# A decoder layer whose feed-forward products are made as seven block products of 2x2 blocks

## What is computed

```python
x = x + rmsnorm(concat(window_attention(...), pool_mix(...)) @ w_out, g_post)
h = rmsnorm(x, g_pre_ffn)
a = jnp.square(jax.nn.relu(h @ w_up))      # w_up   (2048, 8192)
y = x + rmsnorm(a @ w_down, g_post_ffn)    # w_down (8192, 2048)
```

## Time and profile before

| | |
|---|---|
| runs, median (lowest to highest) | 2207.6 us (2205.54 to 2207.78) |
| profiled execution, span | 2207.5 us |
| TensorE busy | 2151.8 us, 97% |
| VectorE, ScalarE, POOL busy | 966.5, 533.8 and 149.3 us |
| mean granted clock of TensorE | 0.979 |
| chain that ended last | TensorE 94%, VectorE 4% |

### The profile page before, as it was taken

How to read it: one execution, slowest core, us unless ns; L and a number is a source line. 1 busy time by engine, 2 the same in 40 slices (tenths; PEclk the granted TensorE clock), 3 DMA queues, 4 the chain that set the end, 5 groups by cost and what they waited for, 6 DMA issues and landing times.

```text
span 2207.5 us, 39376 instructions
## 1 busy us (share of the span) xinstructions
PE 2151.8 (97%) x16878; PEld 2123.3 (96%) x16878; DVE 966.5 (44%) x1212; ACT 533.8 (24%) x743; POOL 149.3 (7%) x135
## 2 busy tenths in 40 slices
PE   7999999999889999999999999999999999999996
PEld 7999989999889999999999999999999999999995
DVE  3455436322574344343434444343344434334446
ACT  5244414222231212121121212112121112212132
POOL 0000023100350000000000000000000000000024
PEclk9999989999889999999999999999999999999996
DMA  5421112522112222222223222222222222222222
GB/s 174 148 64 52 58 58 67 180 86 86 57 48 86 87 90 91 86 86 86 86 85 95 86 86 86 88 90 85 88 86 86 88 93 86 86 86 86 86 67 81
DMA packets 181548, 192.70 MB, mean 87 GB/s; under 512 B 6080, under 2 KB 177480, under 8 KB 180911
## 3 DMA queue, kind: packets, MB, share of 16 engines
q1 hardware_dynamic: 178016, 181.96, 26.2%
q10 hardware_dynamic: 3479, 9.99, 1.2%
HBM read 186.95 MB, written 7.37 MB: 88 GB/s over the span
## 4 chain that ended last, share of the span: by engine, by line
PE 94%; DVE 4%; DMA 0%; issue 0%; ACT 0%; SPq 0%; POOL 0%; DVEq 0%; ACTq 0%; POOLq 0%
PE banks L1271 89%; PE banks L1416 1%; DVE acts_lo L1138 1%; DVE x1T L1213 1%; PE banks L1237 1%; PE banks L1386 1%; DVE x1T L1143 1%; PE banks L1404 1%; DVE w_lo L808 1%; DMA x_tok<-in_x_sample 0%; PE banks L1458 0%; PE banks L1245 0%; PE banks L1457 0%; DVE k_twice L871 0%; DVE x1T L1147 0%
## 5 line engine op out<-in xcount | busy, mean ns | idle before, releaser
L808 DVE TENSOR_TENSOR w_lo<-w_raw,w_hi 128x1024 fp32r<-128x1024 f32 x330 | 421.4, 1277 | 688.6 <-ACT w_hi L545 685.0
L1271 PE MATMUL banks<-acts_hi,w_hi 128*128 128x272 f32 x3232 | 681.2, 292 | 17.3 <-DVE acts_lo L1138 5.3
L1271 PE MATMUL banks<-acts_hi,w_lo 128*128 128x272 f32 x3232 | 674.2, 290 | 0.0
L1271 PE MATMUL banks<-acts_lo,w_hi 128*128 128x272 f32 x3232 | 671.9, 290 | 0.0
L545 ACT ACTIVATE w_hi<-w_raw 128x1024 fp32r<-128x1024 f32 x330 | 349.3, 1059 | 1305.6 <-PE banks L1271 1298.6
L1271 PEld LDWEIGHTS banks<-acts_hi,w_hi 128*128 128x128 f32 x3232 | 512.9, 190 | 24.9 <-issue 14.8
L1271 PEld LDWEIGHTS banks<-acts_lo,w_hi 128*128 128x128 f32 x3232 | 513.6, 191 | 0.0
L1271 PEld LDWEIGHTS banks<-acts_hi,w_lo 128*128 128x128 f32 x3232 | 510.2, 191 | 0.0
L1271 PE MATMUL banks<-mlp_lo,w_hi 128*128 128x272 f32 x2048 | 424.8, 288 | 0.0
L1271 PE MATMUL banks<-mlp_hi,w_hi 128*128 128x272 f32 x2048 | 422.5, 287 | 0.0
L1271 PE MATMUL banks<-mlp_hi,w_lo 128*128 128x272 f32 x2048 | 422.3, 287 | 0.0
(11 more groups left out here) (187 smaller groups left out, 732.6 us busy)
## 6 DMA issues: line engine op xcount, KB each, us to landing
w_raw<-in_w_up SPq DMA_DIRECT2D x128, 512.0 KB, 3.6
w_raw<-in_w_down SPq DMA_DIRECT2D x128, 512.0 KB, 3.3
w_raw<-in_w_in SPq DMA_DIRECT2D x40, 512.0 KB, 3.6
w_raw<-in_w_out SPq DMA_DIRECT2D x32, 512.0 KB, 3.4
x_tok<-in_x_prompt SPq DMA_DIRECT2D x8, 512.0 KB, 9.1
x_tok<-in_x_prompt ACTq DMA_DIRECT2D x4, 1024.0 KB, 8.0
out<-w_raw SPq DMA_DIRECT2D x16, 256.0 KB, 2.6
old_k<-in_cache_k ACTq DMA_DIRECT2D x1, 1024.0 KB, 19.5
```

Of the source, the lines that this page charges most:

```text
L808: nc.vector.tensor_tensor(w_lo[:, k % SPLIT_SLOTS, :], w_raw[:, k % RAW_SLOTS, :], w_hi[:, k % SPLIT_SLOTS, :].bitcast(F32), ALU.subtract) ...
L1271: ins = nc.tensor.matmul(out[:, h, :], w, x[:, h * H:(h + 1) * H], start=first, stop=last)
```

## The change

The two feed-forward products are no longer made chunk by chunk. Each operand is seen as 2x2 blocks: the inner dimension by even and odd tiles of 128, the output columns by the two tiles of a pair, the rows by the two halves of 272. Of each group the four weight blocks b11, b12, b21, b22 and four activation blocks are combined to seven products instead of eight, each with its own high and low parts (Winograd's form of Strassen's scheme):

- POOL makes four differences of weight blocks per group: t1 = b12 - b11, t3 = b22 - b12, t2 = b22 - t1, t4 = b21 - t2 (buffers `t_x`, `t_z`, `t_y`). The sums of activation blocks are made once for the up product by VectorE (`h_sums`), and for the down product by POOL (`activation_sums`).
- For each product N ScalarE copies the weights twice with rounding, once to PSUM (`high_copy`, banks 4 to 7) and once to SBUF (`high_part`); VectorE subtracts the PSUM copy from the weights (`low_part`).
- `take` adds each finished product from its PSUM bank (one of 0 to 3, 272 columns) into the block sums `quads` or `y_sum`. Some products are accumulated on top of what the bank holds, and `taken_before` says which takes TensorE awaits.
- There are two passes. The up pass has 32 groups of 7 products of 8 x 3 matmuls; after each, relu and square (`square_relu`), POOL's sums, rounding (`mlp_high`), rest (`mlp_low`), and two stores to DRAM (`mlp_kept`). The down pass has 8 chunks of 8 groups of 7 products of 4 x 3 matmuls, and reads the parts back (`load_part`). Raw weights have two buffers of 2 MB in the up pass, three of 1 MB in the down pass.
- The input is scaled before the first product (`scale_tiles`), so all tiles are turned and summed before it. x1 is stored to DRAM and read back in the last chunk.
- The loops of the out-projection and the feed-forward are written out; SBUF is laid out by hand.

```diff
+        BANK = (None, 3, None, 2, None, 2, None)
+        GOES_TO = (0, 0, 1, 3, 3, 1, 2)
+        T_NEEDS = {2: 3, 3: 1, 4: 2, 6: 4}
...
+            def load_part(c, i):
+                sp.dma_start(mlp_parts[:, c % 2, i].bitcast(F32),
+                             mlp_kept[c * DOWN_J:(c + 1) * DOWN_J, :, KEPT_AT[i]].rearrange("j p h n -> p j h n")
+                             ).then_inc(mlp_landed[i], 16)
...
+            for g in range(UP_GROUPS):
+                if g > 0:
+                    store_hi(g - 1)
+                    store_lo(g - 1)
...
+            for i in range(NP):
+                sp.wait_ge(product_done, N_UP - NP + i // 2 + 1)
+                load_part(0, i)
...
+            def t4(G):
+                gp.wait_ge(part_hi, NP * G + 3)
+                gp.wait_ge(part_lo, NP * G + 3)
+                gp.wait_ge(t_ready, 4 * G + 3)
+                nc.gpsimd.tensor_tensor(t_of(G, t_y), block_of(G, 1, 0), t_of(G, t_y), ALU.subtract).then_inc(t_ready, 1)
...
+            def high_part(N):
+                if split_free(N):
+                    act.wait_ge(product_done, split_free(N))
+                nc.scalar.activation(split_of(N, 0), weight_of(N), ACT.Copy).then_inc(part_hi, 1)
...
+            for N in range(4, N_ALL):
+                high_copy(N)
+                high_part(N)
+                G, i = divmod(N, NP)
+                if i == 4 and 0 < G < UP_GROUPS:
+                    mlp_high(G - 1)
...
+            for N in range(3, N_UP):
+                take(N)
+                if N < N_UP - 3:
+                    low_part(N + 3)
...
+                if i == 2 and G > 0:
+                    mlp_low(G - 1)
+                if i == 6:
+                    square_relu(G)
...
+            def taken_before(G, i):
...
+                last_group = NP * (G - 1)
+                return (last_group, last_group + 2, NP * G + 1, last_group + 6, NP * G + 3, NP * G + 4, NP * G + 5)[i]
...
+            def strassen_product(N):
+                G, i = divmod(N, NP)
+                pe.wait_ge(part_hi, N + 1)
+                pe.wait_ge(part_lo, N + 1)
+                if taken_before(G, i) > 0:
+                    pe.wait_ge(taken, taken_before(G, i))
...
+                for j in range(pairs):
...
+                    nc.tensor.matmul(out, wh, xh, start=first, stop=False, skip_group_check=not STARTS[i])
+                    nc.tensor.matmul(out, wh, xl, start=False, stop=False, skip_group_check=not STARTS[i])
+                    ins = nc.tensor.matmul(out, wl, xh, start=False, stop=j == pairs - 1, skip_group_check=not STARTS[i])
+                ins.then_inc(product_done, 1)
```

More of the change, by code:

```diff
@@ L40 @@
 UNIT_N = 256
+SB_BASE = 16512
+SB_END = 229344
 POOL_WINDOWS = (2, 4, 8, 16)
@@ L533, in _ @@
+            add(2, KT - 2, sqf_sum, sqf_tmp)
             gp.wait_ge(scale_ready, 4)
@@ L1206, in _ @@
+            for N in range(N_UP, N_ALL):
+                take(N)
+                if N + 4 < N_ALL:
+                    low_part(N + 4)
+                if N == N_UP + 3:
+                    mlp_low(UP_GROUPS - 1)
+            row_scales(3, norm_f)
             dve.wait_ge(scale_ready, 4)
+            for one in x1_moved:
+                dve.wait_ge(one, 32)
             def finish_tiles(kg):
```

740 lines of the change are left out of this document (490 added, 250 removed).

## The result

The changed kernel takes 2095.4 us (median of four runs, 2095.1 to 2096.8) against 2207.7 us before (2205.5 to 2208.5): ratio 0.949, 95% interval 0.948 to 0.951. The forecast was 2091 with 2050 to 2150. The profiled execution has a span of 2095.1 us, 112.4 less than the one before.

The account below looks back on a forecast made before the run. TensorE, busy 97% of the span, was taken as the bound, by its number of matmuls. 2207.5 - 192.3 (matmuls) + 28 (up-pass chain) + 37 (handover) + 10 (between passes) + 1 (tail) = 2091 us, range 2050 to 2150.

Parts of the forecast that it names:

- Step 1: Feed-forward matmuls on TensorE: 1536 fewer at an unchanged 125.2 ns each, -192.3 us.
- I am wrong if the pace of matmuls itself moves: Sign against the forecast: the feed-forward's time per matmul, kept at 125.2 ns, changes.
- Step 2: Down pass: work of VectorE, ScalarE and POOL fits beside TensorE's 1.5 us products, cost 0.
- Step 3: Up pass: one chain across VectorE, POOL and ScalarE makes TensorE wait 0.9 us per group, +28 us.
- The prediction's 0.3: Up-pass chain: overlap in us of a VectorE and POOL operation pair, taking 1.78 and not 2.08.
- Step 4: Handover into the feed-forward: scaled inputs, sums and parts needed first, so it begins in effect at 664, +37 us.
- Step 5: Between up and down pass: first down products wait for parts loaded from DRAM, the seventh late by +10 us.
- Step 6: Tail after the last matmul: a take, two squares and one POOL sum, +1 us.
- A: Rival: everything in the up pass is hidden, only the handovers cost; 2063, down to 2050 us; chance 0.17.
- B: Rival: up-pass chain longer, or down pass short of cover too; 2115 to 2160 us; chance 0.25.
- C: Rival: POOL's differences at twice the price lengthen the chain, 2229 us; decides from 1.85 times; chance 0.11.

Follow-up runs that it names:

- all three edits: Changed kernel with VectorE's rest parts behind take 3, four down parts loaded ahead of group 30's stores, POOL's block sums ahead of its fourth difference: 2072.2 us, 0.938.
- the eight products: Changed kernel with the first product of every group issued twice, so 12288 feed-forward matmuls again: 2264.6 us, 1.026.
- The two bank runs: Kernel before with three successive matmuls into one bank: 2221.6 us, 1.006; control with that weight order but alternating banks: 2207.7 us, 1.000.
- two_terms: Changed kernel without the matmul of low weights by high activations in every feed-forward tile, 7168 matmuls: 1891.4 us, 0.857.
- rest_later: Changed kernel with VectorE's rest parts moved from behind take 2 to behind take 3 in the up pass: 2079.9 us, 0.942.
- sums_first: Changed kernel with POOL's four activation sums ahead of its fourth weight difference instead of behind it: 2099.9 us, 0.951.
- at twice the price: Changed kernel with an extra operation of the same shape on POOL ahead of each weight difference: 2378.4 us, 1.078.

## Why the prediction was right, step by step

The steps, each with what the profiled executions gave (us):

| step | predicted | measured | how |
|---|---|---|---|
| 1 matmuls, count | -192.3 | -192.3 | 1536 x 125.2 ns |
| 1 matmuls, pace | 0 | +7 | 10752 matmuls in products of 3.027 and 1.507: 1353.1 against 1346.1 |
| 2 cover in the down pass | 0 | 0 | 1.507 an interval after the first seven |
| 3 chain of the up pass | +28 | +18.4 | 0.61 a group (21.80 - 21.19), 30 groups |
| 4 handover into it | +37 | +39.1, and +2.4 in group 1 | seventh product ends at 686.7; 5.39 - 3.03 |
| 5 between the passes | +10 | +10 | 1.8 and 6 x (2.87 - 1.507) |
| 6 tail | +1 | +3 | 45.6 from the last matmul to the end, before 42.6 (44.0 in all three edits) |
| sum | -116 | -112.4 | |

The forecast is 4 us off, but its terms are off by 7 (pace), -10 (chain), 4.5 (handover and group 1) and 2 (tail). That they nearly cancel is luck.

**Step 1.** The number of matmuls decides, as the stretches and the eight products show. "I keep 125.2 ns" was wrong: a matmul takes 126.1 ns in the up pass and 125.6 in the down pass. The prediction had said "I am wrong if the pace of matmuls itself moves", and by that sign this term failed; it had named the one bank per product and put it at nothing because no row showed it. The two bank runs show, in the kernel before, 0.7 ns for three in a row. That the bank is the whole cause in the new kernel is argued and not shown: the up pass loses 0.9 ns with 24 in a row, but the down pass, with 12 in a row, loses only 0.4, less than three in a row do. What sets these sizes stays open.

**Step 2** holds, and two_terms measures the room: 1.04 of 1.5 us, at the lower end of the "1.0 to 1.2" for ScalarE. The price of ScalarE's copy into PSUM, which had no row, is nearly that of SBUF: 1.01 for 1024, against 1.04 to 1.06.

**Step 3** has the right mechanism; its size is too large, 0.9 a group instead of 0.61 (0.54 at the sixth product, and 0.07 in it). POOL's 1024 takes 2.4 instead of 2.55, and two of them are in the chain, the second as the block ahead of the rest parts; so the chain is 15.4 and not 15.9. Rest_later and two_terms show the chain from both sides: with the take ahead of the rest parts nothing is left of the wait, and with a third fewer matmuls the sixth product still starts 15.6 us after the first. The mutual waits of VectorE and POOL are the clearest reading of the case: a square of 0.43 takes 2.65, rest parts of 2.13 take 2.82 or 4.25, and each time the end is that of the other's operation plus its own time, less 0.13 of overlap. The prediction's 0.3 is for a pair, in which the two change over twice, so it says nearly the same; the chain has three such changes, and the rule without overlap would make it 0.4 longer and not 0.6. The Trainium skill (SBUF — State Buffer, "Who interferes with whom") has them exclude each other for a whole instruction; the rows agree but for that overlap, and sums_first and rest_later add what follows: moving an operation moves the block, in the first onto VectorE's rest parts and in the second onto POOL, where it costs nothing.

**Step 4** had its points at 623, 631, 641.5 and 685; they came at 623.6, 633.0, 643.6 and 686.7. The 2 us are the way from the last sum to the row scale, 9.4 us where the earlier trace rows had 7.5: the small matmuls that gather the sums take 3.9 us at 0.56 a pair (granted clock 0.50 in the 9.4 us), and before, from 580.80 on, 2.2 at 0.36. The spread behind them took 2.6 both times. What it lacked is the load that waits for `hp_lo`: the prediction followed VectorE's queue and not the memory that its last reader frees.

**Step 5** has the sum, in part by luck. As written its working gives 11.7 us and not 10: the seventh part is there at 20.5 + 6 x 3.2 = 39.7 and wanted at 19 + 6 x 1.5 = 28. A group lasts 21, so the first down product could not want its part before 21, which would give 9.7; and the store of the rest parts stands at 12.7 where step 3 has them ready at 15.5. Measured from the start of the last group, that store is issued at 14.5, the first down product starts at 23.0, 1.8 late, and the next six follow 2.87 apart where the text has 3.2: later and faster than foreseen.

**Step 6**: TensorE is idle 2.8 us ahead of the small matmuls where it idled 1.6, because two squares and a POOL sum stand between. The kernel after, the first small matmuls of the tail:

```profile
2052.31 0.56 PE L1599 MATMUL banks<-ones,sqf_sum 128*128 128x1 f32 x2 [2.83 <-POOL sqf_sum L696]
```

The kernel before at the same place:

```profile
2166.73 0.36 PE L1261 MATMUL banks<-ones,sq_tmp 128*128 128x1 f32 x2
```

The kernel with all three edits, again at the same place:

```profile
2029.54 0.35 PE L1604 MATMUL banks<-ones,sqf_sum 128*128 128x1 f32 x2 [2.87 <-POOL sqf_sum L701]
```

The longer idle time is 1.2 us of the 3. Another 0.9 lie in the pairs: they take 0.56 at once, where the first four took 0.36 before; the granted clock is 0.52 from 2052 to 2062. That is not the change's doing: with three edits all eight full pairs take 0.36 after the same idle time, and from the last matmul to the end it is 44.0 us. The eleven profiled executions with this tail lie between 44.0 and 45.7, so the term is +1.4 to +3.

**The rivals.** A needed the chain gone, which is what rest_later made (2079.9; the pace, the start and the passes keep it above 2063). B did not occur. C was the right mechanism with a wrong threshold: at twice the price the kernel is 8% slower, more than its 2229, since POOL's round of 27.3 us is then longer than the chain.

## What to carry over

Where an added chain crosses several engines once per unit of work, compare its length, not the engines' totals, with what the bound engine has to do meanwhile; then look for the one instruction in the chain that the bound engine waits for and that nothing forces to stand there. Follow not only the queue but also the memory that each last reader frees. When two engines exclude each other, moving an operation moves the wait: it was paid by VectorE's rest parts in sums_first, and TensorE waited, and by POOL's third difference in rest_later, and nobody waited. Arrange the order so that the operation with slack is the one that is held up. And when a total agrees with a theory, look at its parts: the group of two_terms matched for two reasons at once.

## What the runs showed of the hardware

- In the kernel before, matmuls of 272 columns take 125.9 ns with three in a row into one PSUM bank and 125.2 with alternating banks; the order of the weights alone changed nothing (2207.7 us).
- A VectorE operation with both operands in SBUF that starts while POOL's runs ends its own time less 0.13 us after POOL's end: 2.65 instead of 0.43 for 272 columns, 4.25 instead of 2.13 for 1904. The other way round it is the same: POOL's difference of 1024 takes 4.18 instead of 2.41 when the rest parts started 0.22 ahead of it.
- ScalarE's rounding copy of 1024 into PSUM takes 1.01 us, into SBUF 1.04 to 1.06; POOL's difference of 1024 in strided blocks 2.4.
- While TensorE waited for seven transfers of 1.1 MB, its products followed each other 2.87 us apart, 388 GB/s for the transfers (an estimate from their size); the core moved 391 GB/s from 1363 to 1383, in and out together.
- The idle time ahead of the tail's small matmuls does not tell at which clock they run: after 2.83 us they took 0.56 us a pair at once (kernel after), after 2.87 us all took 0.36 (all three edits). After 3.41 us of standing still in two_terms the next product ran at a granted clock of 0.61.
